# The last two value blocks of the experts multiplied token tile by token tile, with the final norm, residual and store inside the experts' block

## The reference, cut to what matters

```
f = peer_ffn(h2, w_pq, sub_keys, u_tab, v_tab)     # product-key experts: sum of 128 gated rows of v_tab per token
x = x + gt2 * rmsnorm(f, g_post_ffn)
# rmsnorm(f, g) = f * rsqrt(mean(f * f) + EPS) * g
```

## Time and profile before

| | |
|---|---|
| runs | 2205.62, 2205.93, 2208.29 us; median 2205.93 us |
| the profiled execution | 2208.48 us, its span 2206.7 us |
| mean granted clock of PE | 0.956 of full speed |
| busy share of the span | PE 91%, weight loads 73%, DVE 63%, ACT 32%, POOL 31% |

### The profile page before, as it was taken

The page is one execution under the profiler, slowest core; times in us unless marked ns, Lnnn a source line. Parts: engine busy times, 40 slices in busy tenths (PEclk is TensorE's granted clock), DMA queues, the critical chain, the costliest instruction groups (busy, mean ns, idle before and its releaser), DMA issues. The chain is left out here.

```text
span 2206.7 us, 28784 instructions
## 1 busy us (share of the span) xinstructions
PE 2018.3 (91%) x10595; PEld 1604.0 (73%) x10595; DVE 1386.9 (63%) x2509; ACT 697.6 (32%) x883; POOL 678.3 (31%) x479
## 2 busy tenths in 40 slices
PE   3999675669789999999999999989999999999995
PEld 2985343444588878888888887868888888888884
DVE  3313354844419987967868896736766666666664
ACT  2010201732113345335434534533222222222221
POOL 1000130001014566556546745633322222222120
PEclk8999877889899999999999999999999999999998
DMA  6314632462114579659848956989988888888881
GB/s 250 125 38 26 215 135 82 153 222 86 57 59 129 165 252 343 227 183 337 299 149 286 340 192 211 342 303 363 345 293 278 297 283 299 280 298 279 294 275 57
DMA packets 217295, 488.20 MB, mean 221 GB/s; under 512 B 31272, under 2 KB 99368, under 8 KB 212464
## 3 DMA queue, kind: packets, MB, share of 16 engines
q1 hardware_dynamic: 177600, 319.13, 44.3%
q0 software_dynamic: 36864, 134.23, 16.8%
q10 hardware_dynamic: 2736, 33.60, 3.8%
HBM read 410.07 MB, written 76.57 MB: 221 GB/s over the span
## 5 line engine op out<-in xcount | busy, mean ns | idle before, releaser
L294 POOL TENSOR_TENSOR u_low<-u_raw,u_high 128x1024 fp32r<-128x1024 f32 x128 | 324.2, 2533 | 298.6 <-ACT u_high L1696 193.5
L1626 PE MATMUL experts_ps<-h2h,u_high 128*128 128x512 f32 x1024 | 408.1, 399 | 7.0 <-POOL u_low L294 7.0
L1652 PE MATMUL experts_ps<-s_vh,s_ah 128*128 128x512 f32 x1024 | 399.4, 390 | 8.6 <-DVE s_al L1898 8.6
L1626 PE MATMUL experts_ps<-h2h,u_low 128*128 128x512 f32 x1024 | 400.3, 391 | 0.0
L1652 PE MATMUL experts_ps<-s_vh,s_al 128*128 128x512 f32 x1024 | 399.3, 390 | 0.0
L1652 PE MATMUL experts_ps<-s_vl,s_ah 128*128 128x512 f32 x1024 | 399.2, 390 | 0.0
L1626 PE MATMUL experts_ps<-h2l,u_high 128*128 128x512 f32 x1024 | 399.1, 390 | 0.0
L1513 POOL DMA_INDIRECT gather_rows<-in_v_tab,expert_index x128 | 154.5, 1207 | 527.3 <-DVE u_raw L1907 503.6
L1896 DVE TENSOR_TENSOR s_vl<-s_vr,s_vh 128x1024 fp32r<-128x1024 f32 x128 | 156.7, 1224 | 209.8 <-ACT s_vh L1720 209.7
L1720 ACT CAST s_vh<-s_vr 128x1024 fp32r<-128x1024 f32 x128 | 134.8, 1053 | 462.7 <-PE experts_ps L1652 445.8
L1652 PEld LDWEIGHTS experts_ps<-s_vh,s_ah 128*128 128x128 f32 x1024 | 192.9, 188 | 49.1 <-issue 8.9
(11 more groups left out here) (327 smaller groups left out, 2591.9 us busy)
## 6 DMA issues: line engine op xcount, KB each, us to landing
u_raw<-in_uT SPq DMA_DIRECT2D x128, 512.0 KB, 4.1
s_vr<-in_v_tab SPq DMA_DIRECT2D x128, 512.0 KB, 4.8
scratch_HG<-s_ar SPq DMA_DIRECT2D x128, 256.0 KB, 4.3
scratch_G<-token_gates ACTq DMA_DIRECT2D x16, 2048.0 KB, 11.1
s_ar<-scratch_HG SPq DMA_DIRECT2D x128, 256.0 KB, 3.8
token_gates<-scratch_G SPq DMA_DIRECT2D x32, 1024.0 KB, 10.3
wa<-in_w_ada SPq DMA_DIRECT2D x12, 2048.0 KB, 9.4
past_k<-in_cache_kT SPq DMA_DIRECT2D x8, 1024.0 KB, 9.1
```

The costliest lines, as they stand in the source:

```text
L294: eng.tensor_tensor(self.low[:, s, :, :], self.raw[:, s, :, :], self.high[:, s, :, :].bitcast(F32), ALU.subtract).then_inc(self.low_done, 1)
L1626: mm = pe.matmul(hP[:, slot, :], w[:, slot, k, :], x[:, k, 0:SEQ], start=(k == 0 and w is u.high and x is m.h2h), stop=(k == KD - 1 and w ...
L1652: mm = pe.matmul(yP[:, y, :], a[:, s, t * P:(t + 1) * P], v[:, s, d], start=(first and s == 0 and a is ah and v is vh), stop=(last and s = ...
```

## The change

`add_residual` is removed as a block of its own. `outputs` now takes the list of blocks; the last group runs only blocks 124 and 125 through it. Blocks 126 and 127 are multiplied in `last_outputs`, which waits for the parts of both, and then finishes token tile 0 in both blocks (12 products), then tile 1, and so on, raising `tile_made` after each. The final norm is done in the experts' block, one tile at a time in the order TAIL = (0, 4, 1, 2, 3): ACT squares a tile when it is there, DVE makes its mean, POOL its root (one 128x1 instruction for each tile), DVE the two long operations, SP the store. DVE issues the mean of the next tile ahead of the two long operations of a tile. The product of the gates moves into DVE's value loop, after block 120.

```diff
+    result = lambda t: yP[:, 2 * t:2 * t + 2, :].rearrange("p a n -> p (a n)") if t < ND else own[:, 0, :]
+    TAIL = (0, NT - 1) + tuple(range(1, NT - 1))
 # gpsimd, after the last fetch
+                for i, t in enumerate(TAIL):
+                    pool.wait_ge(mean_done, i + 1)
+                    pool.tensor_tensor(m.rstd[:, t:t + 1], m.stat[:, t:t + 1], m.mhalf[:, 0:1], ALU.pow).then_inc(root_done, 1)
 # sync, after the last load
+                for i, t in enumerate(TAIL):
+                    sp.wait_ge(added, i + 1)
+                    sp.dma_start(T["y_out"][t * P:(t + 1) * P, :], x1[:, t, :]).then_inc(stored, 16)
+                sp.wait_ge(stored, 16 * NT)
 # tensor
+                def last_outputs(blocks):
+                    pe.wait_ge(al_done, NKEY)
+                    pe.wait_ge(vl_done, NKEY)
+                    for t in range(ND):
+                        for s in blocks:
+                            for y in (2 * t, 2 * t + 1):
+                                mm = output(s, y, stop=(s == blocks[-1]))
+                        mm.then_inc(tile_made, 1)
-                outputs(NGR - 1, False, True)
+                outputs(NGR - 1, range(GB - 2))
+                last_outputs((GB - 2, GB - 1))
 # scalar
+                for i, t in enumerate(TAIL):
+                    if t < ND:
+                        act.wait_ge(tile_made, t + 1)
+                    else:
+                        act.wait_ge(own_done, 1)
+                    if i >= 2:
+                        act.wait_ge(squared, i - 1)
+                    act.activation(junk[:, i % 2, :], result(t), ACT.Square, accum_out=m.stat[:, t:t + 1]).then_inc(squared, 1)
 # vector
                 for n in range(1, NKEY):
                     weigh_values(n)
                     add_row(n - 1)
+                    if n == NKEY - 2 * GB:
+                        dve.wait_ge(res.came, 16 * (2 + NSEQ))
+                        dve.tensor_tensor(gates[:, :, :], gates[:, :, :], spread(res.post[:, :], 1, 2), ALU.mult
+                                          ).then_inc(gate_ready, 1)
...
+                def mean(i):
+                    v = m.stat[:, TAIL[i]:TAIL[i] + 1]
+                    dve.wait_ge(squared, i + 1)
+                    dve.tensor_scalar(v, v, 1.0 / D, EPS, ALU.mult, ALU.add).then_inc(mean_done, 1)
+                dve.wait_ge(gate_ready, 1)
+                mean(0)
+                for i, t in enumerate(TAIL):
+                    if i + 1 < NT:
+                        mean(i + 1)
+                    dve.wait_ge(root_done, i + 1)
+                    dve.scalar_tensor_tensor(result(t), result(t), m.rstd[:, t:t + 1], gates[:, t // ND, :], ALU.mult, ALU.mult
+                                             ).then_inc(stepped, 1)
+                    dve.wait_ge(stepped, i + 1)
+                    dve.wait_ge(res.base_in[t], 16)
+                    dve.tensor_tensor(x1[:, t, :], x1[:, t, :], result(t), ALU.add).then_inc(added, 1)
-        add_residual(nc, m, sem, "res2", res, src, T["y_out"], junk)
```

More of the change, by code:

```diff
@@ L1106, in load @@
             sp.dma_start(self.keep[t], self.base[t * P:(t + 1) * P, :]).then_inc(self.base_in[t], 16)
[L1109 to L1149, removed]
 def mix(nc, m, T, sem, sb, psctx, wide):
@@ L1481, in experts @@
     own_done, h2_rows = sem("own_done"), sem("h2_sample_rows")
+    tile_made, gate_ready, squared, mean_done, root_done, stepped, added, stored = (
+        sem("res2_" + n) for n in ("made", "gate", "sq", "mean", "root", "step", "added", "stored"))
+    TAIL = (0, NT - 1) + tuple(range(1, NT - 1))
     NA, NB, NCC = 5 * NG + 1, 5 * H + 3, 12
@@ L1640, in token_step, with output, outputs @@
                             mm.then_inc(g_made, 1)
-                def outputs(g, first=False, last=False):
-                    for s in range(GB):
+                def output(s, y, start=False, stop=False):
+                    t, d = y // 2, slice((y % 2) * 512, (y % 2 + 1) * 512)
+                    for a, v in ((ah, vh), (al, vh), (ah, vl)):
+                        mm = pe.matmul(yP[:, y, :], a[:, s, t * P:(t + 1) * P], v[:, s, d],
+                                       start=(start and a is ah and v is vh), stop=(stop and v is vl))
+                    return mm
+                def outputs(g, blocks, first=False):
+                    for s in blocks:
                         n = g * GB + s
@@ L1649, in outputs @@
                                 pe.wait_ge(gelu_done, NKEY)
[L1650 to L1654, removed]
-                        mm.then_inc(y_made, 1)
+                            mm = output(s, y, first and s == 0)
+                        mm.then_inc(y_made, 1)
+                def last_outputs(blocks):
+                    pe.wait_ge(al_done, NKEY)
+                    pe.wait_ge(vl_done, NKEY)
+                    for t in range(ND):
+                        for s in blocks:
+                            for y in (2 * t, 2 * t + 1):
+                                mm = output(s, y, stop=(s == blocks[-1]))
+                        mm.then_inc(tile_made, 1)
                 scores(0, 0)
@@ L1685, in _ @@
                 pe.wait_ge(dot_done, SLOTS)
-                outputs(0, True)
+                outputs(0, range(GB), True)
                 with pe.Fori(1, NGR - 1) as g:
-                    outputs(g)
-                outputs(NGR - 1, False, True)
+                    outputs(g, range(GB))
+                outputs(NGR - 1, range(GB - 2))
+                last_outputs((GB - 2, GB - 1))
             @block.scalar
@@ L1929, in _ @@
                 dve.tensor_tensor(own[:, 0, :], own[:, 0, :], own[:, 1, :], ALU.add).then_inc(own_done, 1)
-        src = [yP[:, 2 * t:2 * t + 2, :].rearrange("p a n -> p (a n)") for t in range(ND)] + [own[:, 0, :]]
-        add_residual(nc, m, sem, "res2", res, src, T["y_out"], junk)
+                def mean(i):
[13 more added lines that the diff above has]
+                    dve.tensor_tensor(x1[:, t, :], x1[:, t, :], result(t), ALU.add).then_inc(added, 1)
 @contextmanager
```

## The result

The changed kernel takes 2192.3 us (median of four runs, 2191.36 to 2195.29) against 2206.2 for the kernel before: a ratio of 0.9938, with a 95% interval of 0.9920 to 0.9955. The forecast was 2193.8 us, faster, in a range of 2191.5 to 2197.5. The profiled execution took 2192.93 us.

The account below looks back on a forecast made before the run. PE alone bounds the value stage, then 22.4 us of serial tail follow. The last addition moves from 2203.70 to 2191.57, 12.1 us less; against the median 2205.93 that gives 2193.8 us, range 2191.5 to 2197.5.

Parts of the forecast that it names:

- PE's order costs nothing, its new wait has 7.89 us to spare: PE's last 48 products: same end as before; block 127's parts done at 2165.57, needed at 2173.46.
- The gates are hidden in DVE's loop: DVE after block 120: the 2.29 us product of the gates costs nothing, covered by idle time and the spare 7.89 us.
- DVE's first long operation waits for the sample tile's mean, 5.8 us before PE's end: Start of DVE's tail: that mean, not tile 0's root, delays the first long operation to 2178.54; before, 2191.33.
- DVE's chain of five tiles bounds the tail: New tail: ten long operations at 2.54 us a tile set the end, squares and roots hidden; 0.85.
- One root held by the sample tile's operations costs 0.42 us: POOL's root of tile 1 waits for both SBUF-only operations, making DVE 0.42 us late; upper bound 1.7 us.
- The lower bound: POOL's root of tile 1 gets in between the sample tile's two operations and costs DVE nothing.
- The sum: Tail: the last addition ends at 2191.57 instead of 2203.70, 12.1 us less, 10.9 to 12.6 by the bounds.
- stall without a releaser in the tail: Rival: DVE, ACT or POOL stalls with no semaphore explaining it, 1.3 us extra, 5.8 at most; 2195.1 to 2199.6; 0.09.
- the first square at tile 0's end and not PE's: Rival denied here: ACT's first square starts only when PE ends, 8.16 us later; 2202.0, counted as no change; 0.02.
- the clock at 1.00 to PE's end: Rival denied here: PE's last 48 products at the lower clock, 0.425 us each, 9.5 us more; 2203.3; 0.02.
- Late parts: Rival, slower: PE waits for block 127's parts; lateness beyond 7.9 us moves the tail, measurable loss at 24.4 us; 0.02.
- the new order of the banks: Within the lower-clock rival: products going through PSUM banks tile by tile could lose PE's clock, as far as gaps open.

Follow-up runs that it names:

- Order only: The kernel before with only PE's order in the last two blocks changed, `add_residual` kept; 2207.01 us, ratio 0.9998.
- three blocks: The changed kernel with the sample tile first, each mean directly ahead of its own tile's long operations, and blocks 125, 126 and 127 tile by tile; 2191.3 us.
- four blocks: The changed kernel with the whole last group of four blocks multiplied tile by tile; 2199.66 us, ratio 0.9966.
- one block: The changed kernel with only block 127 multiplied tile by tile; 2198.42 us, ratio 0.9963.
- mean in turn: The changed kernel with each mean directly ahead of its own tile's long operations instead of one tile early; 2197.15 us, ratio 0.9954.

## Why the prediction was right

Step by step, against what the changed kernel's rows show:

- *PE's order costs nothing, its new wait has 7.89 us to spare.* Right. `al` of block 127 ends at 2162.48 and the first of the 48 products starts at 2170.20, so 7.72 us were to spare. (The forecast counted 48 pitches back from the end of PE's last row, which lies 0.16 us behind the start of the first; nothing hangs on it.) Order only shows the order's price, nothing; three blocks still leaves PE without a wait; four blocks shows what happens when the slack is used up, 3.05 us of wait and a clock that falls.
- *The gates are hidden in DVE's loop.* Right: 2.29 us at 2125.46 and no wait of PE. No kernel ran with the gates left in the tail.
- *DVE's first long operation waits for the sample tile's mean, 5.8 us before PE's end.* Right: 5.87.
- *DVE's chain of five tiles bounds the tail.* Right: one block moves its beginning by 4.1 us and the end follows by 4.1.
- *One root held by the sample tile's operations costs 0.42 us.* Wrong in size: it costs nothing. Only this root lasted 1.52 us, as foreseen from the earlier trace rows, but it came to its end at 2179.57, during the sample tile's second operation, 0.4 us after the first, and tile 1 needed it only at 2180.41. The lower bound was the right one. The Trainium skill (SBUF — State Buffer, section "Who interferes with whom") says that a vector instruction with two SBUF inputs contends with a GpSimd instruction that reads SBUF. The 1.52 us of this root, against 0.54 and 0.55 of the three beside operations with one operand in PSUM, agree with it. That the root would hold DVE's addition is not borne out, since that addition started 0.03 us after the first operation's end and took its usual 1.22 us.
- *The sum.* Forecast for the tail 7.23 us, measured 6.68; for the saving 12.1 us, measured 12.68 by the trace, and 13.9 and 12.4 by the runs. The term that was off is that root, with some 0.1 us of smaller gaps. The median of the changed kernel is 1.5 us under the forecast, of which the tail explains 0.55; the rest lies ahead of the changed code or in the spread of the runs, and it brought the result to 0.8 us from the lower edge of the range.

Of the rivals, none occurred: no stall without a releaser in the tail, the first square at tile 0's end and not PE's, and the clock at 1.00 to PE's end. Late parts and a fall of the clock do exist, but need two blocks more: with three blocks PE still did not wait, and four blocks shows both together, at 4.9 us. There the clock fell after a wait, not through the new order of the banks, which order only and the changed kernel went through at the old pace.

## What to carry to other kernels

When a long accumulation is followed by work for each output tile, reorder its last steps so that tiles are finished one after another, and take as many steps into that order as the operands' preparation allows without a wait: the tiles should come no closer together than the slowest engine of the tail needs for one (here 2.5 us with the look-ahead, 3.3 without), and the operands of the last step become due at the first of them. Then the order within the tail decides. What is ready early goes first. A look-ahead that hides a short round trip to another engine was worth 2.86 us where DVE's chain was the bound (mean in turn); where the tiles came far apart (four blocks) it made DVE wait 2.83 us for the mean of a tile that was not yet there, with a finished tile's operations behind it. Read a tail as a distance from the end of the engine ahead of it; that number repeated to 0.02 us where whole runs differed by 3.

## What the runs showed of the hardware that was not expected

- PE's clock fell after a wait of only 3.05 us (four blocks): 1.00 (2.4 GHz) in the rows up to the wait, 0.71 in the 2 us around its restart, then 0.50 (1.2 GHz), and 0.94 in the stretch from 2169 on. The fall showed only behind the restart: the products at 2165.54 and 2165.77 are still 0.23 us apart, those at 2167.42 and 2167.85 are 0.43.
- POOL's gather issued at 2125.82 took 2.74 us where the one before took 1.15; it ran beside the 2.29 us product of the gates, which reads both operands from SBUF. The gather beside the gates took 2.74 us in all eight traces with the gates in the loop. But each of the ten traces, before and order only among them, also has four to seven gathers of 2.88 or 2.89 us between 1490 and 1551, where DVE goes from one operation to the next without a gap; other gathers in the same stretch took 1.15. So the moved gates are not the only thing that comes with a long gather, and what lengthens one is not settled. It cost nothing here: rows are fetched four ahead, and none of DVE's row additions behind it waited.
